# First k-step by operands, and fills, turns, a root and tables moved, in a two-block transformer kernel

## What is computed

```python
def first_block(x, ...):                       # MoBA + differential attention, gated, then SwiGLU
    proj = rms_norm(x, norm_mix_pre_g) @ w_in  # q, k, v of both attentions, two gates
    ya = moba_attention(...)                   # 8 heads of 64, in pairs: rounds 0 to 3
    yb = diff_attention(...)                   # 4 heads, two maps each: rounds 4 to 7
    merged = sigmoid(ga) * (ya @ w_branch_a) + sigmoid(gb) * (rms_norm(yb) @ w_branch_b)
    x = x + rms_norm(merged @ w_out, norm_mix_post_g)
    h = rms_norm(x, norm_ffn_pre_g)            # "FFN 1 second root": of tokens 256 to 511
    return x + rms_norm((silu(h @ w_gate) * (h @ w_up)) @ w_down, norm_ffn_post_g)

def second_block(x, c, ...):                   # gated linear attention (GLA) + dilated attention
    h = rms_norm_2(x, norm1_g) * (1 + sc1) + sh1
    gq, gk, gv, gr, glr, aq, ak, av = split(h @ w_in)
    y_gla = gla_group(gq, gk, gv, log_a, gr)   # a state carried over 4 chunks of 128 tokens here
    y_att = dilated_attention_group(rms(aq), rms(ak), av)  # pairs of heads: rounds 8 to 11
    x = x + g1 * (concat(y_gla, y_att) @ w_out)
    h = rms_norm_2(x, norm2_g) * (1 + sc2) + sh2
    u_gate, u_val = split(causal_depthwise_conv(h @ w_up))
    return x + g2 * ((silu(u_gate) * u_val) @ w_down)
```

## Time and profile before

| | us |
|---|---|
| median of 3 runs | 1373.43 (1372.92 to 1374.91) |
| profiled execution, its own time | 1373.26 |
| its span, first to last instruction | 1371.6 |
| PE busy | 1355.8 |
| granted TensorE clock | 1.00 throughout |

### The profile page before, as it was taken

One profiled execution on the slowest core, in us unless ns is written; L12 is line 12 of the kernel. 1 busy time (PEld: TensorE's weight loads), 2 busy tenths in 40 slices (PEclk: granted clock), 3 DMA queues, 4 the chain that ended last, 5 costly groups with the idle time before them and its releaser, 6 DMA issues.

```text
span 1371.6 us, 19384 instructions
## 1 busy us (share of the span) xinstructions
PE 1355.8 (99%) x6846; PEld 1106.6 (81%) x6846; DVE 881.1 (64%) x1479; ACT 589.4 (43%) x984; POOL 57.5 (4%) x119
## 2 busy tenths in 40 slices
PE   9999999999999999999999999999999999999999
PEld 7777777778988888888887688777798888888887
DVE  6667676678777777774337977766576566565221
ACT  5455545554452323323223735666354444443221
POOL 0000000000001211120100000000000000000000
PEclk9999999999999999999999999999999999999999
DMA  6222212213315555555443112111212322233332
GB/s 208 92 77 77 75 64 77 77 62 123 103 63 192 194 196 191 192 188 172 128 142 118 47 62 77 62 62 63 77 58 92 103 95 92 98 101 115 87 97 88
DMA packets 42871, 147.08 MB, mean 107 GB/s; under 512 B 5440, under 2 KB 5952, under 8 KB 42816
## 3 DMA queue, kind: packets, MB, share of 16 engines
q1 hardware_dynamic: 34848, 120.37, 27.0%
q0 software_dynamic: 7824, 25.70, 5.6%
q10 hardware_dynamic: 144, 0.26, 0.1%
HBM read 143.69 MB, written 2.10 MB: 106 GB/s over the span
## 4 chain that ended last, share of the span: by engine, by line
PE 90%; DVE 6%; ACT 2%; issue 1%; DMA 0%; DVEq 0%; SPq 0%; ACTq 0%; POOLq 0%
PE bank L664 60%; PE bank L844 13%; PE bank L682 4%; PE bank L783 3%; PE bank L870 2%; PE bank L960 2%; PE bank L891 1%; PE bank L909 1%; PE bank L1130 1%; DVE w_lo L1940 1%; PE bank L912 1%; ACT w_hi L1326 0%; DVE xT L2442 0%; DVE xT L2255 0%; PE bank L1251 0%
## 5 line engine op out<-in xcount | busy, mean ns | idle before, releaser
L1940 DVE TENSOR_TENSOR w_lo<-raw,w_hi 128x1024 fp32r<-128x1024 f32 (+1 forms) x223 | 266.6, 1196 | 154.4 <-ACT w_hi L1326 153.5
L1326 ACT ACTIVATE w_hi<-raw 128x1024 fp32r<-128x1024 f32 (+1 forms) x223 | 230.5, 1035 | 287.3 <-PE bank L664 262.1
L664 PE MATMUL bank<-h_hi,w_hi 128*128 128x512 f32 x864 | 343.4, 397 | 3.2 <-DVE h_lo L2489 1.3
L664 PE MATMUL bank<-h_hi,w_lo 128*128 128x512 f32 x864 | 336.7, 390 | 0.0
L664 PE MATMUL bank<-h_lo,w_hi 128*128 128x512 f32 x864 | 336.5, 389 | 0.0
L664 PEld LDWEIGHTS bank<-h_hi,w_hi 128*128 128x128 f32 x864 | 162.1, 188 | 43.5 <-issue 3.9
L664 PEld LDWEIGHTS bank<-h_hi,w_lo 128*128 128x128 f32 x864 | 162.2, 188 | 34.3
L664 PEld LDWEIGHTS bank<-h_lo,w_hi 128*128 128x128 f32 x864 | 162.3, 188 | 33.9 <-issue 1.7
L664 PE MATMUL bank<-f_hi,w_lo 128*128 128x512 f32 x352 | 136.9, 389 | 0.0
L664 PE MATMUL bank<-f_hi,w_hi 128*128 128x512 f32 x352 | 136.9, 389 | 0.0
L664 PE MATMUL bank<-f_lo,w_hi 128*128 128x512 f32 x352 | 136.9, 389 | 0.0
(11 more groups left out here) (366 smaller groups left out, 1936.2 us busy)
## 6 DMA issues: line engine op xcount, KB each, us to landing
raw<-in_w_up SPq DMA_DIRECT2D x66, 512.0 KB, 3.3
ada<-in_w_ada POOLq DMA_DIRECT2D x96, 256.0 KB, 3.1
raw<-in_w_mix SPq DMA_DIRECT2D x47, 512.0 KB, 3.3
raw<-in_w_down SPq DMA_DIRECT2D x32, 512.0 KB, 3.5
raw<-in_w_in SPq DMA_DIRECT2D x24, 512.0 KB, 3.2
raw<-in_w_gate SPq DMA_DIRECT2D x22, 512.0 KB, 3.3
raw<-in_w_out SPq DMA_DIRECT2D x16, 512.0 KB, 3.2
raw<-in_w_down SPq DMA_DIRECT2D x16, 384.0 KB, 3.3
```

The source lines that it names most:

```text
L664: last = pe.matmul(to[:, :], wt[:, slot, k, :], act_[:, rhs0 + k, :], start=(k == first and n == 0), stop=(k == K - 1 and n == 2))
L1326: act.activation(w_hi[:, s, k0:K, :], raw[:, s, k0:K, :], ACT.Copy).then_inc(hi_ready[s], 1)
L1940: dve.tensor_tensor(w_lo[:, s, k0:K, :], raw[:, s, k0:K, :], w_hi[:, s, k0:K, :].bitcast(F32), ALU.subtract).then_inc(split_ready[s], 1)
```

## The change

Six edits; no matmul is added or taken away.

1. Start. `first_values` does the first k-step operand by operand, over four banks: first the products that need only `y_hi` and `w_hi`, then `y_lo`, then `w_lo`. The first 8 of the 322 columns of `cols` are loaded apart by ACT's queue ahead of its half tile; the other 314 come behind all of `x` on SP's queue, and ACT and DVE wait for them (`lam_in`) before they use them.
2. Round 0. PE does two steps of the fill ahead of the wait for `qk_ready` and the scores; the turns move by two.
3. Round 7. The last turn moves from step 20 to 22, values and squares by two as well.
4. FFN 1. PE sums the squares of the second half within step 3 of the loop, not after step 4; two filler steps go to the end. ACT takes the root before `rounded_pair(0, 3)`, DVE `pair_scaled(1, 0)` before `pair_rest(0, 3)`.
5. GLA. One fill step goes from chunk 1 to chunk 0. On DVE `dilated_distances(0, 0)` goes from chunk 1 to 2, `dilated_distances(0, 1)` from the head of chunk 3 behind the last `chunk_gate`, and `normed_k(0)` inside it. In round 8 the sum for the key norm comes one step later.
6. Round 11. `pair_values` comes after step 19, not 20.

```diff
 TURNS = {4: (9, 9, 17, 23), 5: (9, 9, 21, 28)}
-LAST_TURNS = (9, 9, 15, 20)
+FIRST_TURNS = (11, 11, 19, 25)
+LAST_TURNS = (9, 9, 15, 22)
...
 DILATED_TURNS = {24: (4, 9, 11, 15, 19, 20), 21: (3, 8, 8, 13, 13, 18)}
-OWN_VALUES = 20
+OWN_VALUES = 19
...
-THIRDS = ((0, 0, 0, 4, 0, 2, 1, 1, 1, 1, 1, 1, 1, 1, 0, 0), (0, 0, 0, 2, 2, 1, 1, 2, 1, 0, 0, 1, 0, 0, 0, 0))
-SECOND_SUM_AT = (4, 5)
+THIRDS = ((0, 0, 0, 4, 0, 2, 1, 1, 1, 1, 1, 1, 0, 0, 0, 0), (0, 0, 0, 2, 2, 1, 1, 2, 1, 0, 0, 1, 0, 0, 0, 0))
+SECOND_SUM_AT = ((3, 3), (5, 0))
...
-            sp.dma_start(cols[:, :], a["cols"]).then_inc(vec_in, 16)
             sp.dma_start(xT[:, 0:1, :], a["x"][:, 0:1, :]).then_inc(first_x_in, 16)
...
             x_load(6)
+            sp.dma_start(cols[:, KD:], a["cols"][:, KD:]).then_inc(lam_in, 16)
             sp.dma_start(lamv[:, :, :], a["lam"]).then_inc(lam_in, 16)
...
                     step(1, i)
-                    if i == SECOND_SUM_AT[b]:
+                    if (i, 0) == SECOND_SUM_AT[b]:
                         sum_of_second_half()
                     for n in range(THIRDS[b][i]):
+                        if n and (i, n) == SECOND_SUM_AT[b]:
+                            sum_of_second_half()
                         if third == 0:
...
+            def first_values(banks):
+                pe.wait_ge(xg_hi, 1)
+                pe.wait_ge(first_half_hi, 1)
+                for m, (xt, wt) in enumerate(((y_hi, w_hi), (y_lo, w_hi), (y_hi, w_lo))):
+                    if m == 1:
+                        pe.wait_ge(xg_ready, 1)
+                    if m == 2:
+                        pe.wait_ge(first_half_lo, 1)
+                    for r in range(NT):
+                        pe.matmul(banks[r][:, :], xt[:, 0, P * r:P * r + P],
+                                  wt[:, 0, 0:4, :].rearrange("p a b -> p (a b)"), start=(m == 0), stop=False)
             def value_products(n, banks):
...
                 if n == 0:
-                    pe.wait_ge(first_half_lo, 1)
-                for kk in range(2):
+                    first_values(banks)
+                for kk in range(1 if n == 0 else 0, 2):
                     if kk == (1 if n == 0 else 0):
...
                 steps = KU * len(ROUNDS[i][1])
-                squares, turn0, turn1, turn2 = LAST_TURNS if i == 7 else TURNS[len(ROUNDS[i][1])]
+                squares, turn0, turn1, turn2 = (FIRST_TURNS if i == 0 else LAST_TURNS if i == 7
+                                                else TURNS[len(ROUNDS[i][1])])
+                begun = 0 if i else 2
                 if i == 0:
+                    fill(0, 0, begun)
                     pe.wait_ge(qk_ready, 2)
...
                     pair_values(i - 1)
-                fill(i, 0, squares)
+                fill(i, begun, squares)
                 if i >= 5:
...
                 else:
-                    fill(i, turn2, 22)
+                    fill(i, turn2, 24)
                     pair_values(7)
-                    fill(i, 22, 25)
+                    fill(i, 24, 27)
                     pair_squares(7)
-                    fill(i, 25, steps)
+                    fill(i, 27, steps)
...
                 if c < NCH - 1:
-                    project(6 + 3 * c if c else 8, 9 + 3 * c)
+                    project((8, 10, 12)[c], (10, 12, 15)[c])
                 if c == 2:
...
                 turned, turn0, norm_q, turn1, norm_k, turn2 = DILATED_TURNS[steps]
+                norm_k += 1 if i == 8 else 0
                 p = i - 8
...
+            act.dma_start(cols[:, 0:KD], a["cols"][:, 0:KD]).then_inc(vec_in, 16)
             act.dma_start(raw[:, 0, 0:4, :], a["w_mix"][0:1, :, 0:4 * P].rearrange("t p n -> (t p) n")
...
                 split_hi(s)
+            act.wait_ge(lam_in, w.next(lam_in, times=2))
             tile_done(act, 8)
...
             x_squares(0, 1)
+            inverse_rms_of_half(1)
             rounded_pair(0, 3)
-            inverse_rms_of_half(1)
             x_squares(0, 2)
...
             dve.tensor_tensor(sqacc[:, :], gate_b[:, 0, :], gate_b[:, 1, :], ALU.add).then_inc(first_sum, 1)
-            dve.wait_ge(lam_in, w.next(lam_in))
+            dve.wait_ge(lam_in, w.next(lam_in, times=2))
             for n in range(2):
...
             pair_to_x(0, 3)
-            pair_rest(0, 3)
             skip_last_square()
             pair_scaled(1, 0)
+            pair_rest(0, 3)
             pair_to_x(1, 0)
...
                     dve.wait_ge(gs_ready, w.next(gs_ready))
-                if c == NCH - 1:
-                    dilated_distances(0, 1)
                 if c >= 1:
...
                     chunk_gate(c - 1, (lambda: normed_q(0)) if c == 2 else None)
-                if c == 1:
+                if c == 2:
                     dve.wait_ge(seen_ln, 1)
                     dilated_distances(0, 0)
-                if c == 2:
                     split_lo(0)
-            normed_k(0)
             dve.wait_ge(gy_done, w.next(gy_done))
-            chunk_gate(NCH - 1)
+            chunk_gate(NCH - 1, lambda: normed_k(0))
+            dilated_distances(0, 1)
             split_lo(1)
```

## The result

The changed kernel takes 1366.99 us (median of 5 executions, 1366.73 to 1367.36), the kernel before 1373.43 (1372.92 to 1374.91). The ratio is 0.9948, 95% interval 0.9937 to 0.9959. The profiled execution took 1367.36 with a span of 1365.7; before it was 1373.26 and 1371.6. A second series gave 1366.92 beside 1374.66 (0.9945, 0.9931 to 0.9958). That is 0.5% less. The forecast was 1367.2: the time was right. Its six terms were not all right, that of the start turned out to be something a single trace can't give, and the sum is as near as it is partly because two errors cancel: in this pair of traces the start gave 0.6 less than forecast and FFN 1 0.3 more. One of the prediction's own signs of being wrong came true as well: the second tile starts at 12.92, later than 12.8.

What follows compares the result with a forecast made beforehand. PE was taken as the bound, busy 1355.8 of 1371.6 us, so only its waits could be gained: 0.7 + 0.85 + 1.2 + 1.5 + 1.4 + 0.45 = 6.1, from 1373.26 to 1367.2. Range for 8 in 10: 1365.9 to 1369.6.

Steps and rivals of the forecast that it cites:

- One of the prediction's own signs of being wrong: At the start: the forecast is wrong if the second tile starts later than 12.8.
- 1, the start: First k-step and table loads: PE and the second tile start earlier, 0.7 us gained, bounds 0.3 to 0.95.
- the second tile then decides: At the start: the second tile's `w_lo`, slack 0.44, limits the gain; tile at 12.4 with a wait of some 0.5.
- The clock rival: At the start: the new order lets PE's clock fall to 1.2 GHz, 0.23 more per matmul, up to 1389; chance 0.02.
- 2, 3 and 6: Rounds 0, 7 and 11: PE's waits for `qk`, `probs` and `y_lo` covered by moved steps, 0.85, 1.2 and 0.45 us gained.
- 4, FFN 1: FFN 1: earlier sum and root, DVE closes two idles, filler covers a `w_lo` wait; 1.5 us gained, bounds 0.8 to 1.9.
- Its three waits: FFN 1: PE's two waits for `h_lo` (0.6 and 0.4) and one for `w_lo` of L1937 (0.5), 2.1 in all.
- 5, GLA and round 8: GLA and round 8: moved steps cover `gstate` and `next_k`, tables move on DVE; 1.4 us gained, bounds 0.3 and 1.9.
- the tail on DVE: End of GLA: `normed_k(0)` and the last table behind the last `gyf` take 0.2 from the wait before the first dilated scores.
- The slack at O1's bank: Round 8: 0.2 of slack at a bank freed for the turned values; if gone, up to 1.5 comes back.
- The waits come back on DVE: Rival: DVE holds PE in FFN 1 and GLA, giving 0.8 and 0.6 there, sum 4.6, time 1368.7; chance 0.2.
- The small table is no faster than the large: Rival at the start: the small table holds ACT's queue as long as the large one; start gives 0.3, time 1367.6; chance 0.07.

Runs made afterwards that it cites:

- `half_first`: The changed kernel with the two loads on ACT's queue exchanged, half tile of the weights first, small table second: 1368.27 us beside 1374.11 for the kernel before.
- `start_undone`: The changed kernel with its start put back (old order of the first k-step, table in one piece heading SP's queue): 1368.12 us beside 1374.11.
- `ffn_pe_only`: The changed kernel with ACT's root and DVE's scaling in FFN 1 back in their old order, PE's order kept: 1368.88 us.
- `round7_only`: The kernel before with only round 7's last turn, values and squares moved two steps later: 1373.33 us against 1373.96, ratio 0.9992.
- `order_only`: The changed kernel with the order by operands kept but the table loaded in one piece heading SP's queue: 1367.82 us beside 1374.11.

## Why the prediction was right, and where it was not

**1, the start: mis-sized from one trace.** Forecast 0.7; at the third tile 0.0 to 1.1 in the five traces of this start, in the medians 0.6 to 1.9, of which the clock has a share that is not told apart. Three steps of it failed.

The first: "The new 4 KB load delays the issue of ACT's half tile by one issue (some 0.4), but that tile is needed only after `y_hi`": the issue was 0.4 later, the landing 2.0 later in the first trace (`w_hi` had to wait 1.63), 1.1 in the second, and this, not `y_hi`, started PE. In the better executions PE began at 6.39 to 6.43 and the second tile at 11.95 to 12.11, better than the 12.4 I gave, since with the small table on ACT's queue the half tile on SP's comes up to 1.8 sooner.

The second step was to take "Before, PE starts at 7.51" and the second tile at 13.12 as the kernel's own: in that trace the half tile on SP's queue landed in 4.9 where all other traces of this arrangement show 5.7 to 6.0, and its products were all fast. It was a good draw, and luck for the forecast of the time, which starts from it; the median of 1373.43 is the lowest of the five series of this kernel (up to 1374.66).

The third step was the bound: "the second tile then decides", with a wait of some 0.5 for its `w_lo`. That `w_lo` was ready at 12.82 in the first trace of the changed kernel and at 11.87 in the second, 0.1 ahead of PE, which came to the tile at 12.92 and 11.95 with its matmuls in a row: PE's own start was the bound.

**The clock rival: right in kind, wrong in side and size.** I had the clock as something that the change might spoil, "from 27 matmuls on". I read it as 1.00, "that is 2.4 GHz, from the start", which is wrong in that very trace: its first 18 ones are 0.21 apart, the last four follow 0.11 apart, and its first clock record begins at 5.12. It was the old start that ran products at 1.2 GHz, for 8 to 14 matmuls and 1.5 to 3 us in two traces (and, of the arrangements tried with 22 ones, `half_first`). No trace of the kernel before itself shows it, but its clock does: of 46 executions beside the experiments, 13 have a mean granted clock of 0.999, and all 13 are above 1374.5 (one more, 1376.92, reads 0.949). A rise that comes late does not show in this mean; that of `start_undone` is 1.000. What my forecast left out is the gain: in none of the five traces of the changed start were the first products slow, and the two series of the changed kernel spread over 1.0 or less where the five of before spread over 1.9 to 3.7. With the changed start it is rarer, not gone: of 24 executions with the changed start and 22 ones, one (1370.68 in `ffn_pe_only`) reads 0.999.

**2, 3 and 6: right** to 0.04 (0.89, 1.22, 0.43). These are waits of PE with one producer, one filler of 1.36 or 0.68, and a known distance to the next wait. `round7_only` shows for one of them that it stands alone and adds.

**4, FFN 1: too small, 1.82 for 1.5.** (Its three waits, "2.1 in all", are 2.3 by its own rule.) The mechanism was right (DVE closes its idles, one `h_lo` stays), but the sum contradicted it. If the second `h_lo` is still waited for, PE is as much earlier behind it as DVE is: the gain there is DVE's, not that of the wait that goes. I added 0.7 for the first wait and 0.15 for a small one, where DVE's own 1.0 stood two sentences before. DVE came from 387.64 to 384.35, which less the shift of 2.16 is 1.13; the other 0.69 of the 1.82 is the third wait, for `w_lo` (0.65). DVE's 1.13 is its two idles, 0.90, and some 0.2 that I put down to two dependent pairs that no longer follow each other directly, which no run shows by itself. Undoing ACT's and DVE's order alone took 1.12 of it back, which is this 1.13.

**5, GLA and round 8: right in the sum, 1.45 for 1.4.** `gstate` gave 0.69 (0.6), `next_k` in round 8 0.68 (0.6), the tail on DVE nearly nothing (0.2), and the 0.4 at the third state came back, not at `gon` as I had it but just ahead of it at `next_k`. The slack at O1's bank held.

**The other rivals.** "The waits come back on DVE" did not happen: 1.82 and 1.45 where it had 0.8 and 0.6. "The small table is no faster than the large" was wrong in its first part: 3.1 us to land for 4 KB is indeed no less than the 3.0 for 161 KB, but `y_hi` started at 4.23 instead of 5.27 since `x` no longer stood behind the table, and beside `order_only` the split gave 0.4 or more at the third tile. The rule of the Trainium skill that I had weighed ("DMA: Bandwidth & Descriptors", Rules for kernel authors), that small transfers are mostly overhead, agrees with the 3.1 against 3.0; it did not tell what the split did to the transfers around it.

## What to carry to other kernels

Where PE is the bound, a wait is worth what its producer gains, if the next wait on the same producer stays: take the shift of the producer at the last wait that is left, not the sum of the waits that go. A step of the bound engine moved in front of a wait was worth its forecast to within 0.1 at each of six places (rounds 0, 7 and 11, the third wait of FFN 1, `gstate` and `next_k`); a long step of another engine belongs into that engine's own idle time just behind the operation that is waited for. The first 15 us of a kernel are not to be read from one trace: with one and the same start the second tile came up to 3 us apart there, by transfers and by the clock, while the edited stretches behind repeated within 0.07.

## What the hardware showed that I had not expected

- PE's ones run at half rate from the start (22 in 5.03 us, 0.21 apart) and in some executions go over to 0.11 after 14 to 21 of them (22 in 4.09), though the granted clock of these stretches reads 1.00. The distance between matmuls shows the rate; the column does so only from the trace's first clock record on. It read 0.50 at 8 to 11 us in `round7_only`, but 1.00 in `start_undone` and `half_first`, where the matmuls were just as far apart (0.43).
- PE ran its first 7 to 14 products of 512 columns 0.43 apart in four traces, after standing 0.62, 1.43, 1.99 and 3.56 us behind the ones; after 0.94 to 1.8 us in five others, and after less than 0.9 in the remaining five, they ran 0.23 apart. The time that PE stands does not tell the two apart by itself.
- 256 KB on ACT's queue and 256 KB on SP's queue, issued within a few us of each other, land in 2.9 to 3.8 and 5.7 to 6.0 us (4.9 in one of six traces), or, with a 4 KB load ahead on ACT's queue, in 4.0 to 5.2 and 4.1 to 5.2. The same 4 KB ahead on SP's queue do not do this (one trace: 2.9 and 5.7).
